# Keys and values of block 2 as seven products of half the columns, interleaved with the queries

## The chip, the cores and the metric

One core of one Trainium2 chip. The time is device microseconds (us) of one execution. Before the change three runs took 1544.66, 1544.93 and 1547.16 us, median 1544.93 us.

## The reference, cut to what matters

The program is two transformer blocks over 256 tokens of width 1,024, all in float32. Block 2 begins with a mixer whose input is projected to eight parts, among them the queries, keys and values of an attention; later comes a mixture of 64 experts.

```python
def mixer_block(u, cos, sin, w_in, conv_w, q_norm_g, k_norm_g, w_conv_out, w_attn_out, w_o):
    B, S, _ = u.shape
    proj = u @ w_in
    cb, cc, cx, q, k, v, gc, ga = split_columns(proj)
    ...
    q = rmsnorm(q.reshape(B, S, N_HEADS, HEAD_DIM), q_norm_g)
    k = rmsnorm(k.reshape(B, S, N_KV_HEADS, HEAD_DIM), k_norm_g)
    v = v.reshape(B, S, N_KV_HEADS, HEAD_DIM)
```

The queries have 1,024 columns, keys and values 256 each; `cc`, `cx`, `cb`, `gc`, `ga` have 1,024 each.

## The kernel before

**Seven products.** A product of a 256 x 1,024 activation with a 1,024 x 1,024 weight is cut into 2 x 2 blocks (tokens in halves of 128, the inner dimension in halves of 512, columns in halves of 512) and computed with seven block products in place of eight. With activation blocks a11, a12, a21, a22 (first index tokens) and weight blocks b11 to b22, DVE makes activation sums s1 = a21 + a22, s2 = s1 - a11, s3 = a11 - a21, s4 = a12 - s2 and weight sums t1 = b12 - b11, t2 = b22 - t1, t3 = b22 - b12, t4 = b21 - t2. PE makes product 1 = a11 b11, 2 = a12 b21, 5 = s1 t1, 6 = s2 t2, 7 = s3 t3, 3 = s4 b22, 4 = a22 t4, each four matmuls of 512 columns into one PSUM bank. The result blocks come from running sums: u2 = 1 + 6, u3 = u2 + 7, c22 = u3 + 5, c12 = u2 + (5 + 3), c21 = u3 + 4, c11 = 1 + 2. Product 2 is added by PE onto product 1 in its bank and 3 onto product 5, so product 2 waits until ACT has copied product 1 away, and product 3 waits until DVE has formed c22. Product 4 takes the bank of product 6 and waits for u2.

**The stretch of the change.** After block 1's last products (line 1432) the input of block 2 is normed, turned by PE (`norm_turn`, line 887) and scaled into `hT`, first for the first 128 tokens, then for the second. Keys and values, the unit `kv2` (512 columns, 2 MB), come as plain products in four parts of four matmuls (`part`, line 928): two parts on the first tokens, two on the second. DVE and ACT empty the two banks (`empty2`). Then come the queries as seven products in the order 1, 5, 6, 7, 2, 3, 4 (`q_seven`, line 1494, units `q0`, `q1`), then `cc` in the order 5, 1, 6, 7, 2, 3, 4 (`seven_product`, line 1553), then `cx`, `cb` with the attention between their products, then `gc`, `wco`, `ga`, `wao` (line 1558) and `wo`.

**Who sets the order.** Each engine runs a fixed list; `SCHEDULE2` gives the sequence of stages, and inside a stage it is the order of the calls. For the queries DVE runs `q_first_w_sums` (t1, t3, lines 2763 and 2764) and then `q_sums`: s1, s3, s2, t2, s4, t4 (lines 2771 to 2780), the rotation tables (2490), the norm and rotation of the keys (2511 to 2505), `cc`'s t1 (2554), `cc`'s t2 (2677), and only then the queries' u2, u3, c22 (all line 2799), `cc`'s t3 and t4 (2680, 2683), and c12 and c21.

**The ring.** Weights of 2 MB come through four slots. SP issues each unit's load (line 688) as soon as PE has counted up `dense_used` for the unit that had the slot before. `kv2` has slot 0, `q0` 1, `q1` 2, `cc0` 3, and `cc1` takes slot 0 after `kv2`. `kv2` is released in `q_seven`, right behind the first matmul of product 1:

```python
                        if product == 1 and c == 0:
                            release_last()
```

`release_last` waits until the last product of `kv2` is in its bank. `cc0` and `cc1` together hold b11 to b22 of `cc`, so its t1 needs both. The experts' 400 MB then come through 11 slots in the same way; the loads of the first ones wait for the end of the attention, of `wao` and of `wo`.

Of the kernel before, what the change touches and what calls it, by code (L numbers as in the profile page):

```python
# [168 lines left out]
SCHEDULE2 += [("part", "kv2", _q) for _q in range(4)] + [("seven", 0, 0)]  # L169
# [32 lines left out]
ORDER_UP = [1, 5, 6, 7, 2, 3, 4]  # L202
W_SUMS_UP = ["t1", "t3", "t2", "t4"]
# [17 lines left out]
def copied7(g):  # L221

    return 2 * SETS7 + g + (3 if g else 2)
# [22 lines left out]
def up_bank(m):  # L246

    return 4 * (m % 2)
# [10 lines left out]
def two_blocks(nc, t, out):  # L259

    with ExitStack() as ctx:
# [152 lines left out]
        q_t1, q_t3 = (flat1[:, at:at + 2048].rearrange("p (c n) -> p c n", c=4) for at in (0, 2048))  # L414
        q_x = flat1[:, 4096:6144].rearrange("p (j c s) -> p j c s", j=4, c=4)
# [61 lines left out]
        def up_seven_bank(m, product):  # L477
            return ps[:, up_bank(m) + BANK7[product], :]

# [117 lines left out]

        conv_mid, cbz_ready = sem("conv_mid"), sem("cbz_ready")
# [276 lines left out]
        def _(pe):  # L875
# [600 lines left out]
            def q_seven():  # L1476

                for n in ("q0", "q1"):
                    pe.wait_ge(dense_loaded[RING_SLOT[UNIT[n]]], dense_loads(UNIT[n]))
                b11, b12, b21, b22 = q_columns()  # L1480
                for product in ORDER_UP:
                    if product in (5, 6, 7, 4):
                        pe.wait_ge(w_sums7_ready, count7(-1, W_SUMS_UP, {5: "t1", 6: "t2", 7: "t3", 4: "t4"}[product]))
                    if product in (5, 6, 7, 3):
                        pe.wait_ge(x_sums7_ready, count7(-1, X_SUMS7, {5: "s1", 6: "s2", 7: "s3", 3: "s4"}[product]))
                    if product == 2:
                        pe.wait_ge(seven_copied, 2 * UP_SETS + 2)
                    if product in (3, 4):
                        pe.wait_ge(seven_sums, count7(-1, SUMS7, {3: "c22", 4: "u2"}[product]))
                    for c in range(4):  # L1490
                        lhs = {1: hT[:, c, 0:P], 2: hT[:, 4 + c, 0:P], 4: hT[:, 4 + c, P:S], 5: q_x[:, 0, c, :],
                               6: q_x[:, 1, c, :], 7: q_x[:, 2, c, :], 3: q_x[:, 3, c, :]}[product]
                        rhs = {1: b11, 2: b21, 3: b22, 4: w_sum_b, 5: q_t1, 6: b12, 7: q_t3}[product][:, c, :]
                        last = mm(ps[:, 4 + BANK7[product], :], lhs, rhs, start=(c == 0 and product not in (2, 3)),  # L1494
                                  stop=(c == 3), skip_group_check=True)
# [71 lines left out]
            def release_q():  # L1567

                pe.wait_ge(seven_filled, count7(-1, ORDER_UP, 4))
                pe.sem_inc(dense_used, 2)  # L1570
# [7 lines left out]
            for kind, a, q in SCHEDULE2:  # L1578
                if kind == "part":
                    if q % 2 == 0:  # L1580
                        wait_hT(16 + 2 * q)
                    part(a, hT, True, q)
                    if q == 0:
                        norm_turn(2, xn2, 1)
                elif kind == "product":
# [4 lines left out]
                elif kind == "seven":  # L1590
                    q_seven()
# [334 lines left out]
        def _(dve):  # L1926
# [548 lines left out]
            norm_rows(2, xn2, 0)  # L2475
            norm_take(2, 0)
            dve.wait_ge(ff_down, 5)
# [67 lines left out]
            def first_w_sums(g, part=(1, 3)):  # L2545
# [9 lines left out]
                if 3 in part:  # L2555
                    if SEVENS[g] == "cx":
                        dve.wait_ge(seven_filled, count7(-1, ORDER_UP, 4))
# [112 lines left out]
            def cc_w_sums(names):  # L2670

                b11, b12, b21, b22 = columns7(SET["cc"])
                for name in names:
                    if name == "t2":
                        dve.wait_ge(seven_filled, count7(-1, ORDER_UP, 5))
                        dve.wait_ge(w_sums7_ready, count7(0, W_SUMS_CC, "t1"))
                        v.tensor_tensor(q_t1, b22, w_sum_a, ALU.subtract).then_inc(w_sums7_ready, 1)
                    if name == "t3":
                        dve.wait_ge(seven_filled, count7(-1, ORDER_UP, 7))
                        v.tensor_tensor(q_t3, b22, b12, ALU.subtract).then_inc(w_sums7_ready, 1)  # L2680
# [85 lines left out]
            def q_sums():  # L2766
# [25 lines left out]
            def q_sum(name, dst, r, product):  # L2792

                dve.wait_ge(seven_filled, count7(-1, ORDER_UP, product))
                if name == "u2":
                    dve.wait_ge(seven_copied, 2 * UP_SETS + 2)
# [4 lines left out]
            dve.wait_ge(hT_act, 20)  # L2801
            q_first_w_sums()
            for kind, a, q in SCHEDULE2:
                if kind == "part":
                    if q % 2 and PRODUCTS[PROD[a]][1][q // 2] == "D":
                        empty2(a, q // 2)
                elif kind == "product":
# [232 lines left out]
        def _(act):  # L3040
# [208 lines left out]
            def empty2(name, bank):  # L3249
                b = filled_bank(name, bank)  # L3250
                if name == "kv2":
# [24 lines left out]
            for kind, a, q in SCHEDULE2:  # L3276
                if kind == "part":
                    if q % 2 and PRODUCTS[PROD[a]][1][q // 2] == "A":
                        empty2(a, q // 2)
                elif kind == "product":  # L3280
# [8 lines left out]
                elif kind == "seven":  # L3289
                    act.wait_ge(bank_emptied_dve, emptied("D", PROD["kv2"], 0))  # L3290
# [158 lines left out]
```

## Time and profile before

| what | value |
|---|---|
| median of three runs | 1544.93 us |
| profiled execution | 1545.07 us |
| its span on the core | 1543.2 us |
| PE busy | 1247.8 us (81%) |
| DVE busy | 549.4 us (36%) |
| ACT busy | 246.7 us (16%) |
| DMA, mean over the span | 325 GB/s |

The span is what the profiler saw of instructions; 1.87 us of the execution lie outside it. A float32 matmul shows as two records, so four matmuls read "x8". Start and end times are from the span's start. A bracket behind a timeline row is the idle time of that engine before it and what ended it.

### The profile page before, as it was taken

The numbers are of one execution on the slowest core, as the hardware profiler recorded it, in microseconds if no ns is written. First come the engines' busy times: TensorE is split into PE (matmuls) and PEld (weight loads), VectorE is DVE, ScalarE is ACT, GpSimd is POOL, SyncE is SP. The second block draws the span as 40 slices with busy tenths as digits, with TensorE's granted clock in tenths as the row PEclk, the third lists the DMA queues.
The fourth block names the chain that finished last, engine by engine and source line by source line (L and its number), as shares of the span: only waits on it lengthen the run. The fifth ranks groups of instructions, "written<-read, shape, count | busy, mean of one in ns | idle before, by whom it ended". The sixth has DMA issues, their size and how long they took to land.

```text
span 1543.2 us, 18891 instructions
## 1 busy us (share of the span) xinstructions
PE 1247.8 (81%) x8005; PEld 706.6 (46%) x8005; DVE 549.4 (36%) x1115; ACT 246.7 (16%) x710; POOL 18.2 (1%) x30
## 2 busy tenths in 40 slices
PE   8999999999999999996765775775676576577477
PEld 5665899944699544542232232232232233223223
DVE  6644578795756667421111111111111111111111
ACT  2434213211234101211010010010000001001001
POOL 2000000000000000100000000000000000000000
PEclk9999999999999999998888898788798789788889
DMA  9631746406433686999999999999999999999997
GB/s 305 217 111 55 244 153 217 162 30 217 163 112 113 236 303 237 374 429 428 429 429 429 428 429 428 428 429 428 429 429 428 428 429 428 429 429 429 429 426 327
DMA packets 93859, 501.53 MB, mean 325 GB/s; under 512 B 6845, under 2 KB 34865, under 8 KB 68464
## 3 DMA queue, kind: packets, MB, share of 16 engines
q1 hardware_dynamic: 93040, 500.00, 79.9%
q0 software_dynamic: 768, 0.85, 0.2%
q8 instruction: 33, 0.54, 0.1%
q14 instruction: 18, 0.15, 0.0%
HBM read 499.78 MB, written 1.05 MB: 325 GB/s over the span
## 4 chain that ended last, share of the span: by engine, by line
PE 58%; DMA 39%; DVE 2%; issue 1%; ACT 1%; SPq 0%; DVEq 0%
DMA arena<-in_w 38%; PE ps L1754 18%; PE ps L1329 8%; PE ps L1558 6%; PE ps L1553 4%; PE ps L1366 3%; PE ps L928 2%; PE ps L1139 2%; PE ps L933 2%; PE ps L978 2%; PE ps L1494 2%; PE ps L1654 1%; PE ps L1279 1%; PE ps L1432 1%; PE ps L955 0%
## 5 line engine op out<-in xcount | busy, mean ns | idle before, releaser
L1754 PE MATMUL ps<-arena,hT 128*32 128x512 f32 x1984 | 277.8, 723 | 252.7 <-DMA arena<-in_w 252.7
L1754 PEld LDWEIGHTS ps<-arena,hT 128*32 128x32 f32 x1984 | 69.2, 130 | 460.8 <-issue 319.3
L3006 DVE TENSOR_TENSOR moe_hid<-moe_hid,ps 64x512 f32<-64x512 f32 x32 | 22.1, 690 | 480.8 <-ACT moe_hid L3407 480.8
L1776 PE MATMUL ps<-arena,moe_turned 128*32 128x512 f32 x1024 | 118.3, 601 | 28.0 <-DVE moe_turned L3008 27.9
L1734 PEld LDWEIGHTS ps<-sel,h 128*128 128x128 f32 x992 | 113.2, 192 | 24.1 <-issue 24.1
L3407 ACT ACTIVATE moe_hid<-ps 64x512 f32<-64x512 f32 x32 | 18.8, 588 | 655.9 <-PE ps L1754 650.3
L1734 PE MATMUL ps<-sel,h 128*128 128x64 f32 x992 | 117.2, 276 | 0.0
L3391 ACT ACTIVATE hT<-ps,gcol 128x64 f32<-128x64 f32 x252 | 55.0, 328 | 156.8 <-PE ps L1734 156.8
L3008 DVE COPY moe_turned<-ps 128x512 f32<-128x512 f32 x32 | 22.1, 692 | 161.8 <-PE ps L1765 161.8
L1776 PEld LDWEIGHTS ps<-arena,moe_turned 128*32 128x32 f32 x1024 | 32.9, 110 | 88.7 <-issue 72.0
L1329 PE MATMUL ps<-arena 128*128 128x128 f32 x640 | 73.1, 275 | 0.0
L1329 PEld LDWEIGHTS ps<-arena 128*128 128x128 f32 x640 | 72.3, 192 | 0.0
L3010 DVE COPY moe_y<-ps 128x512 f32<-128x512 f32 x32 | 22.1, 692 | 125.0 <-PE ps L1776 125.0
L1785 PE MATMUL ps<-moe_y,moe_turned 64*128 64x512 f32 x256 | 63.6, 615 | 0.8 <-DVE moe_y L3010 0.8
L1558 PE MATMUL ps<-arena 128*128 128x512 f32 x144 | 63.7, 593 | 0.0
L1329 PE MATMUL ps<-hT,arena 128*128 128x128 f32 x480 | 55.4, 275 | 0.0
L1329 PEld LDWEIGHTS ps<-hT,arena 128*128 128x128 f32 x480 | 54.5, 192 | 0.0
L1553 PE MATMUL ps<-arena 128*128 128x128 f32 x384 | 44.7, 275 | 0.0
L1553 PEld LDWEIGHTS ps<-arena 128*128 128x128 f32 x384 | 44.3, 192 | 0.8 <-issue 0.5
L1366 PE MATMUL ps<-arena 128*128 128x512 f32 x96 | 42.4, 593 | 0.0
L1558 PEld LDWEIGHTS ps<-arena 128*128 128x128 f32 x144 | 27.0, 190 | 33.2 <-issue 32.0
L1785 PEld LDWEIGHTS ps<-moe_y,moe_turned 64*128 64x128 f32 x256 | 22.0, 186 | 42.8 <-issue 41.1
(499 smaller groups left out, 1427.3 us busy)
## 6 DMA issues: line engine op xcount, KB each, us to landing
arena<-in_w SPq DMA_DIRECT2D x182, 2048.0 KB, 29.4
arena<-in_w_in SPq DMA_DIRECT2D x18, 2048.0 KB, 9.1
arena<-in_w_up SPq DMA_DIRECT2D x22, 1024.0 KB, 9.0
arena<-in_w SPq DMA_DIRECT2D x17, 1024.0 KB, 12.9
arena<-in_w_down SPq DMA_DIRECT2D x5, 2048.0 KB, 13.5
arena<-in_w_out SPq DMA_DIRECT2D x2, 2048.0 KB, 15.2
arena<-in_w_conv_out SPq DMA_DIRECT2D x2, 2048.0 KB, 7.7
arena<-in_w_attn_out SPq DMA_DIRECT2D x2, 2048.0 KB, 11.9
```

Source lines behind the costliest of these rows:

```text
L928: last = mm(ps[:, at, :], xT[:, c, bank * P:(bank + 1) * P], w[:, c, :], start=(c == 0), stop=(c == KC - 1))
L933: last = mm(o, w[:, c, q * P:(q + 1) * P], xT[:, c, :], start=(c == 0), stop=(c == KC - 1))
L978: last = mm(ps[:, BANK1[product], :], lhs[:, c, :], rhs[:, c, :], start=(c == 0 and product != 3), stop=(c == 3), skip_group_check=True)
L1329: last = mm(up_seven_bank(m, product)[:, q * P:(q + 1) * P], wb[:, c, q * P:(q + 1) * P], xs[:, c, :], start=(new and q == 0 and c == 0), ...
L1366: return mm(ps[:, bank, :], x, w, start=(i == 0), stop=(i == NPAIR - 1))
L1553: last = mm(bank7(g, product)[:, m * P:(m + 1) * P], wb[:, c, m * P:(m + 1) * P], xs[:, c, :], start=(new and m == 0 and c == 0), stop=(c ...
L1558: last = mm(bank7(g, product), xs[:, c, :], wb[:, c, :], start=(new and c == 0), stop=(c == 3), skip_group_check=True)
L1734: last = mm(ps[:, GT, c * 2 * CAP:(c + 1) * 2 * CAP], hview[:, half, c, :], sel[:, half, :], start=(half == 0), stop=(half == 1))
L1754: last = mm(ps[k * CAP:(k + 1) * CAP, UP, :], x[:, c, (k % 2) * CAP:(k % 2 + 1) * CAP], w[:, at:at + DE], start=(c == 0), stop=(c == KC - 1))
L1776: last = mm(ps[k * CAP:(k + 1) * CAP, DN, :], a[:, m * 64 + (k % 2) * CAP:m * 64 + (k % 2 + 1) * CAP], w[:, at:at + 512], start=(m == 0), ...
L1785: last = mm(ps[:, 2 * half + n, :], sT[rows, half * P:(half + 1) * P], moe_y[rows, :], start=False, stop=False, skip_group_check=True)
L3391: return a_(xg[:, c, :], ps[:, bank, c * 2 * CAP:(c + 1) * 2 * CAP], ACT.Copy, scale=gcol[:, 3, c:c + 1])
```

## The change

Keys and values get seven products too, of 256 columns each: keys are the first column half, values the second. The activation sums s1 to s4 are those of the queries, made once, and now made ahead of the queries' weight sums. The weight sums of `kv2` (four of 128 x 1,024) are made by DVE during block 1's last products, into room of their own. PE runs, by `kv_and_queries`: kv 1, half of queries 1, the turn of the second tokens, the other half of queries 1, kv 2, then kv 5, 6, 7, queries 2, kv 3, kv 4, queries 5, 6, 7, 3, 4. ACT copies products 1 of both away first and takes the first tokens' keys and the queries' c11; DVE forms the other key and value blocks (`kv_sum`). `kv2` is now released behind the first matmul of the queries' product 5. The core of the diff:

```diff
-SCHEDULE2 += [("part", "kv2", _q) for _q in range(4)] + [("seven", 0, 0)]
+SCHEDULE2 += [("seven", 0, 0)]
...
+ORDER_Q, ORDER_KV = [1, 2, 5, 6, 7, 3, 4], [1, 2, 5, 6, 7, 3, 4]
...
-            def q_seven():
...
+            def kv(product):
...
+                if product == 1:
+                    u = UNIT["kv2"]
+                    pe.wait_ge(dense_loaded[RING_SLOT[u]], dense_loads(u))
+                    wait_bank(PROD["kv2"], 0)
+                    wait_bank(PROD["kv2"], 1)
+                b11, b12, b21, b22 = kv_columns()
+                if product in (5, 6, 7, 4):
+                    pe.wait_ge(kv_summed, count1(KV_SUMS, {5: "t1", 6: "t2", 7: "t3", 4: "t4"}[product]))
+                if product in (5, 6, 7, 3):
+                    pe.wait_ge(x_sums7_ready, count7(-1, X_SUMS7, {5: "s1", 6: "s2", 7: "s3", 3: "s4"}[product]))
+                if product == 2:
+                    pe.wait_ge(seven_copied, KV_COPIED)
+                if product in (3, 4):
+                    pe.wait_ge(kv_summed, count1(KV_SUMS, {3: "c22", 4: "u2"}[product]))
+                for c in range(4):
+                    lhs = {1: hT[:, c, 0:P], 2: hT[:, 4 + c, 0:P], 4: hT[:, 4 + c, P:S], 5: q_x[:, 0, c, :],
+                           6: q_x[:, 1, c, :], 7: q_x[:, 2, c, :], 3: q_x[:, 3, c, :]}[product]
+                    rhs = {1: b11, 2: b21, 3: b22, 4: kv_t["t4"], 5: kv_t["t1"], 6: kv_t["t2"], 7: kv_t["t3"]}[product][:, c, :]
+                    last = mm(kv_bank(product), lhs, rhs, start=(c == 0 and product not in (2, 3)), stop=(c == 3),
+                              skip_group_check=True)
+                last.then_inc(kv_filled, 1)
+
+            def queries(product, chunks=range(4)):
+
+                if product in (1, 5) and 0 in chunks:
+                    u = UNIT["q0" if product == 1 else "q1"]
...
-                        if product == 1 and c == 0:
-                            release_last()
...
+                    pe.wait_ge(x_sums7_ready, count7(-1, X_SUMS7, {5: "s1", 6: "s2", 7: "s3", 3: "s4"}[product]))
+                if product == 2:
+                    pe.wait_ge(seven_copied, KV_COPIED + 1)
...
+                    if product == 5 and c == 0:
+                        pe.wait_ge(kv_filled, len(ORDER_KV))
+                        pe.sem_inc(dense_used, 1)
+                if 3 in chunks:
                     last.then_inc(seven_filled, 1)
+
+            def kv_and_queries():
+
+                wait_hT(16)
+                kv(1)
+                queries(1, (0, 1))
+                norm_turn(2, xn2, 1)
+                queries(1, (2, 3))
+                kv(2)
+                wait_hT(20)
+                for product in (5, 6, 7):
+                    kv(product)
+                queries(2)
+                kv(3)
+                kv(4)
+                for product in (5, 6, 7, 3, 4):
+                    queries(product)
...
-                    q_seven()
+                    kv_and_queries()
...
+                x, y = {"t1": (b12, b11), "t3": (b22, b12), "t2": (b22, kv_t["t1"]), "t4": (b21, kv_t["t2"])}[name]
+                v.tensor_tensor(kv_t[name], x, y, ALU.subtract).then_inc(kv_summed, 1)
+
+            kv_w_sum("t1")
             norm_take(2, 0)
+            for name in ("t3", "t2", "t4"):
+                kv_w_sum(name)
...
-            def empty2(name, bank):
...
-                    v.tensor_copy(z2[:, 0, 1024:1280], b[:, 0:256])
-                    v.tensor_copy(v2[:, 0, :], b[:, 256:512]).then_inc(bank_emptied_dve, 1)
+            def kv_sum(name):
+
+                dst, r, product = {"u2": (kv_u2, kv_u2, 6), "u3": (kv_u3, kv_u2, 7), "c22": (v2[:, 1, :], kv_u3, 5),
+                                   "c12": (v2[:, 0, :], kv_u2, 3), "c21": (z2[:, 1, 1024:1280], kv_u3, 4)}[name]
+                dve.wait_ge(kv_filled, count1(ORDER_KV, product))
+                if name == "u2":
+                    dve.wait_ge(seven_copied, KV_COPIED)
+                else:
+                    dve.wait_ge(kv_summed, count1(KV_SUMS, {"u3": "u2", "c22": "u3", "c12": "u2", "c21": "u3"}[name]))
+                done = bank_emptied_dve if name == "c21" else kv_summed
+                v.tensor_tensor(dst, r, kv_bank(product), ALU.add).then_inc(done, 1)
...
+                dve.wait_ge(hT_act, 20)
                 v.tensor_tensor(q_x[:, 0], a21, a22, ALU.add).then_inc(x_sums7_ready, 1)
                 v.tensor_tensor(q_x[:, 2], a11, a21, ALU.subtract).then_inc(x_sums7_ready, 1)
                 dve.wait_ge(x_sums7_ready, count7(-1, X_SUMS7, "s1"))
                 v.tensor_tensor(q_x[:, 1], q_x[:, 0], a11, ALU.subtract).then_inc(x_sums7_ready, 1)
+                dve.wait_ge(x_sums7_ready, count7(-1, X_SUMS7, "s2"))
+                v.tensor_tensor(q_x[:, 3], a12, q_x[:, 1], ALU.subtract).then_inc(x_sums7_ready, 1)
+                q_first_w_sums()
+                for name in ("u2", "u3", "c22"):
+                    kv_sum(name)
                 dve.wait_ge(w_sums7_ready, count7(-1, W_SUMS_UP, "t3"))
                 v.tensor_tensor(b12, b22, q_t1, ALU.subtract).then_inc(w_sums7_ready, 1)
-                dve.wait_ge(x_sums7_ready, count7(-1, X_SUMS7, "s2"))
-                v.tensor_tensor(q_x[:, 3], a12, q_x[:, 1], ALU.subtract).then_inc(x_sums7_ready, 1)
                 dve.wait_ge(w_sums7_ready, count7(-1, W_SUMS_UP, "t2"))
                 v.tensor_tensor(w_sum_b, b21, b12, ALU.subtract).then_inc(w_sums7_ready, 1)
+                kv_sum("c12")
+                kv_sum("c21")
                 turn_tables()
                 keys()
                 first_w_sums(0, (1,))
...
-            dve.wait_ge(hT_act, 20)
-            q_first_w_sums()
...
-            def empty2(name, bank):
-                b = filled_bank(name, bank)
-                if name == "kv2":
-                    a_(z2[:, 1, 1024:1280], b[:, 0:256], ACT.Copy)
-                    a_(v2[:, 1, :], b[:, 256:512], ACT.Copy).then_inc(bank_emptied_act, 1)
...
+                    act.wait_ge(kv_filled, count1(ORDER_KV, 1))
+                    a_(kv_u2, kv_bank(1), ACT.Copy).then_inc(seven_copied, 1)
+                    act.wait_ge(seven_filled, count7(-1, ORDER_Q, 1))
+                    a_(r1_, ps[:, 4 + BANK7[1], :], ACT.Copy).then_inc(seven_copied, 1)
+                    act.wait_ge(kv_filled, count1(ORDER_KV, 2))
+                    a_(z2[:, 0, 1024:1280], kv_bank(2), ACT.Copy).then_inc(bank_emptied_act, 1)
+                    act.wait_ge(seven_filled, count7(-1, ORDER_Q, 2))
+                    a_(z2[:, 0, 0:512], ps[:, 4 + BANK7[2], :], ACT.Copy).then_inc(seven_copied, 1)
                     act.wait_ge(bank_emptied_dve, emptied("D", PROD["kv2"], 0))
...
-                    act.wait_ge(seven_filled, count7(-1, ORDER_UP, 1))
-                    a_(r1_, ps[:, 4 + BANK7[1], :], ACT.Copy).then_inc(seven_copied, 1)
                     act.wait_ge(seven_sums, count7(-1, SUMS7, "c22"))
                     head_squares(1, range(4, 8))
-                    act.wait_ge(seven_filled, count7(-1, ORDER_UP, 2))
-                    a_(z2[:, 0, 0:512], ps[:, 4 + BANK7[2], :], ACT.Copy).then_inc(seven_copied, 1)
-                    act.wait_ge(seven_copied, 2 * UP_SETS + 3)
+                    act.wait_ge(seven_copied, KV_COPIED + 2)
                     head_squares(0, range(4))
                     act.wait_ge(seven_sums, count7(-1, SUMS7, "c12"))
```

PE where `kv2` is released, the last two parts of keys and values and the start of the queries, before:

```order
L928 MATMUL ps<-arena,hT 128x512 [waits bank_emptied_dve,hT_act,hT_dve]
L928 MATMUL ps<-arena,hT 128x512 x7
L1494 MATMUL ps<-arena,hT 128x512 [waits dense_loaded2,dense_loaded1]
L1494 MATMUL ps<-arena,hT 128x512 [waits bank_filled]
L1494 MATMUL ps<-arena,hT 128x512 x2
L1494 MATMUL ps<-arena 128x512 [waits x_sums7_ready,w_sums7_ready]
L1494 MATMUL ps<-arena 128x512 x3
```

and now, from the queries' product 2 on (L1533 is the queries, L1511 keys and values):

```order
L1533 MATMUL ps<-arena,hT 128x512 [waits seven_copied]
L1533 MATMUL ps<-arena,hT 128x512 x3
L1511 MATMUL ps<-arena 128x256 [waits kv_summed,x_sums7_ready]
L1511 MATMUL ps<-arena 128x256 x3
L1511 MATMUL ps<-arena,hT 128x256 [waits kv_summed]
L1511 MATMUL ps<-arena,hT 128x256 x3
L1533 MATMUL ps<-arena 128x512 [waits x_sums7_ready,w_sums7_ready,dense_loaded2]
L1533 MATMUL ps<-arena 128x512 [waits kv_filled]
L1533 MATMUL ps<-arena 128x512 x2
```

The wait on `bank_filled`, behind which `kv2` is released, became one on `kv_filled`; the queries' products 1 and 2, which but for one matmul stood behind it, now stand in front of it.

PE at the end of the queries, products 7, 2, 3, 4, before:

```order
L1494 MATMUL ps<-arena 128x512 [waits x_sums7_ready,w_sums7_ready]
L1494 MATMUL ps<-arena 128x512 x3
L1494 MATMUL ps<-arena,hT 128x512 [waits seven_copied]
L1494 MATMUL ps<-arena,hT 128x512 x3
L1494 MATMUL ps<-arena 128x512 [waits seven_sums,x_sums7_ready]
L1494 MATMUL ps<-arena 128x512 x3
L1494 MATMUL ps<-arena,hT 128x512 [waits seven_sums,w_sums7_ready]
L1494 MATMUL ps<-arena,hT 128x512 x3
```

and now, products 7, 3, 4:

```order
L1533 MATMUL ps<-arena 128x512 [waits x_sums7_ready,w_sums7_ready]
L1533 MATMUL ps<-arena 128x512 x3
L1533 MATMUL ps<-arena 128x512 [waits seven_sums,x_sums7_ready]
L1533 MATMUL ps<-arena 128x512 x3
L1533 MATMUL ps<-arena,hT 128x512 [waits seven_sums,w_sums7_ready]
L1533 MATMUL ps<-arena,hT 128x512 x3
```

Product 2 went from between 7 and 3 to an earlier place; the wait of product 3 on `seven_sums` (for c22) now stands right behind product 7.

DVE from the last step of the keys' rotation, before (slot 0 is `dense_loaded0`; `moe_turned` is u2, `moe_hid` is u3, then c22):

```order
L2504 TENSOR_TENSOR arena<-arena 128x2x128 [waits dve_step]
L2505 TENSOR_TENSOR arena<-arena 128x2x128
L2554 TENSOR_TENSOR arena<-arena 128x2048 [waits dense_loaded0,dense_loaded3,dve_step]
L2677 TENSOR_TENSOR arena<-arena 128x2048 [waits w_sums7_ready,seven_filled]
L2799 TENSOR_TENSOR moe_turned<-moe_turned,ps 128x512 [waits seven_copied,seven_filled]
L2799 TENSOR_TENSOR moe_hid<-moe_turned,ps 128x512 [waits seven_sums,seven_filled]
L2799 TENSOR_TENSOR arena<-moe_hid,ps 128x512 [waits seven_sums,seven_filled]
```

and now:

```order
L2573 TENSOR_TENSOR arena<-arena 128x2x128 [waits dve_step]
L2574 TENSOR_TENSOR arena<-arena 128x2x128
L2629 TENSOR_TENSOR arena<-arena 128x2048 [waits dense_loaded0,dense_loaded3,dve_step]
L2752 TENSOR_TENSOR arena<-arena 128x2048 [waits w_sums7_ready,seven_filled]
L2880 TENSOR_TENSOR moe_turned<-moe_turned,ps 128x512 [waits seven_copied,seven_filled]
L2880 TENSOR_TENSOR moe_hid<-moe_turned,ps 128x512 [waits seven_sums,seven_filled]
L2880 TENSOR_TENSOR arena<-moe_hid,ps 128x512 [waits seven_sums,seven_filled]
```

Nothing moved here: the queries' u2, u3 and c22 stand behind `cc`'s t1, which waits for `cc1` in slot 0, as before.

## Rows read from the trace of the kernel before

**Rows 1.** The profile page, its 40 slices of 38.6 us: DMA share in tenths.

```profile
DMA  9631746406433686999999999999999999999997
```

**Rows 2.** Busy time by stretch: PE, PEld, DVE, ACT, POOL; then PE clock, DMA share, GB/s.

```profile
550.00:600.00 50.00, 50.00 (x119) 22.10 (x118) 32.08 (x29) 3.68 (x6) 0.00 (x0) 1.00 0.60 216
```

**Rows 3.** Chain of waits, 360 to 440 us and whole span: start, length, what, matmul records.

```profile
372.42 3.43 PE ps L928 x8
...
376.74 10.30 PE ps L928 x24
387.04 24.03 PE ps L1494 x56
411.07 25.01 PE ps L1553 x224
...
506.36 93.68 PE ps L1558 x218
```

**Rows 4.** Chain of waits, line 933: matmuls of 256 columns.

```profile
47.24 13.81 PE ps L933 x64
```

**Rows 5.** DMA issues of line 688: those of kv2 and q0, and the landing of each.

```profile
L688 SPq DMA_DIRECT2D arena<-in_w_in x1: 551/551/551, 353.6 to 353.6; - x1
L688 SPq DMA_DIRECT2D arena<-in_w_in x1: 546/546/546, 363.8 to 363.8; - x1
...
DMA to landing us min/median/max: 8.0/8.0/8.0
```

**Rows 6.** Issue of cc1 (line 688); landing of it, of the one at 411.2, of eleven (300 to 480 us).

```profile
387.16 0.54 SPq L688 DMA_DIRECT2D arena<-in_w_in  x1
...
DMA to landing us min/median/max: 9.2/9.2/9.2
...
DMA to landing us min/median/max: 9.6/9.6/9.6
...
DMA to landing us min/median/max: 7.8/8.7/14.4
```

**Rows 7.** Timeline of DVE, 352 to 412 us; start, length, instruction, idle before.

```profile
364.26 0.75 DVE L1952 TENSOR_SCALAR arena<-arena,rstd 128x1024 f32<-128x1024 f32 x1
...
372.46 0.69 DVE L2407 TENSOR_TENSOR arena<-arena,ps 128x512 f32<-128x512 f32 x1 [4.47 <-PE ps L1432]
...
377.95 2.29 DVE L2763 TENSOR_TENSOR arena<-arena 128x2048 f32<-128x2048 f32 x1 [0.49 <-ACT hT L3071]
...
382.36 0.42 DVE L2529 COPY arena<-ps 128x256 f32<-128x256 f32 x1
...
396.45 2.29 DVE L2554 TENSOR_TENSOR arena<-arena 128x2048 f32<-128x2048 f32 x1 [1.72 <-DMA arena<-in_w_in]
...
401.06 0.68 DVE L2799 TENSOR_TENSOR moe_turned<-moe_turned,ps 128x512 f32<-128x512 f32 x1
...
402.64 0.69 DVE L2799 TENSOR_TENSOR arena<-moe_hid,ps 128x512 f32<-128x512 f32 x1
```

**Rows 8.** Timeline of ACT, 352 to 412 us: scaling of the second tokens.

```profile
376.78 1.14 ACT L3071 ACTIVATE hT<-ps,gcol 128x128 f32<-128x128 f32 x4 [2.54 <-PE ps L887]
```

**Rows 9.** Timeline of PE, experts: three of the up products, line 1754.

```profile
701.60 7.08 PE L1754 MATMUL ps<-arena,hT 128*32 128x512 f32 x64 [1.76 <-DMA arena<-in_w]
...
730.80 9.69 PE L1754 MATMUL ps<-arena,hT 128*32 128x512 f32 x64 [11.03 <-DMA arena<-in_w]
...
760.32 8.59 PE L1754 MATMUL ps<-arena,hT 128*32 128x512 f32 x64 [8.93 <-DMA arena<-in_w]
```

**Rows 10.** Busy time by stretch, columns as in rows 2: where the clock changes.

```profile
722.00:723.00 1.00, 0.00 (x0) 0.00 (x0) 0.36 (x2) 0.00 (x0) 0.00 (x0) 0.74 1.00 426
756.00:757.00 1.00, 0.00 (x0) 0.00 (x0) 0.00 (x0) 0.00 (x0) 0.00 (x0) 0.80 1.00 426
736.00:737.00 1.00, 1.00 (x16) 0.35 (x12) 0.00 (x0) 0.00 (x0) 0.00 (x0) 0.94 1.04 442
```

**Rows 11.** Chain of waits, whole span: the last of 27 such gaps, behind its transfer.

```profile
1495.02 9.93 PE ps L1754 x64
```

More of the change, by code:

```diff
@@ L202 @@
 ORDER_UP = [1, 5, 6, 7, 2, 3, 4]
+ORDER_Q, ORDER_KV = [1, 2, 5, 6, 7, 3, 4], [1, 2, 5, 6, 7, 3, 4]
+KV_COPIED = 2 * UP_SETS + 2
+KV_SUMS = ["t1", "t3", "t2", "t4", "u2", "u3", "c22", "c12", "c21"]
 W_SUMS_UP = ["t1", "t3", "t2", "t4"]
@@ L221, in copied7 @@
 def copied7(g):
-    return 2 * SETS7 + g + (3 if g else 2)
+    return 2 * SETS7 + g + (4 if g else 3)
 def x_sum_wo(name):
@@ L414, in two_blocks @@
         q_t1, q_t3 = (flat1[:, at:at + 2048].rearrange("p (c n) -> p c n", c=4) for at in (0, 2048))
+        kv_t = {n: flat0[:, at:at + 1024].rearrange("p (c n) -> p c n", c=4)
+                for n, at in (("t1", 0), ("t2", 7168), ("t3", 8192), ("t4", 9216))}
+        kv_u2, kv_u3 = moe_y[:, 0:256], moe_y[:, 256:512]
         q_x = flat1[:, 4096:6144].rearrange("p (j c s) -> p j c s", j=4, c=4)
@@ L478, in up_seven_bank, with kv_bank, kv_columns @@
             return ps[:, up_bank(m) + BANK7[product], :]
+        def kv_bank(product):
+            return ps[:, BANK7[product], 0:256]
+        def kv_columns():
+            w = dense_slot("kv2").rearrange("p (c n) -> p c n", c=KC)
+            return w[:, 0:4, 0:256], w[:, 0:4, 256:512], w[:, 4:8, 0:256], w[:, 4:8, 256:512]
         def bank7(g, product):
@@ L1473, in attend @@
                         pe.sem_inc(attn2_done, 1)
-            def q_seven():
-                for n in ("q0", "q1"):
-                    pe.wait_ge(dense_loaded[RING_SLOT[UNIT[n]]], dense_loads(UNIT[n]))
-                b11, b12, b21, b22 = q_columns()
[L1481 to L1495, printed above, removed]
-                        if product == 1 and c == 0:
-                            release_last()
-                    last.then_inc(seven_filled, 1)
@@ new lines, in queries @@
+            def queries(product, chunks=range(4)):
+                if product in (1, 5) and 0 in chunks:
+                    u = UNIT["q0" if product == 1 else "q1"]
+                    pe.wait_ge(dense_loaded[RING_SLOT[u]], dense_loads(u))
+                b11, b12, b21, b22 = q_columns()
+                if product in (5, 6, 7, 4):
+                    pe.wait_ge(w_sums7_ready, count7(-1, W_SUMS_UP, {5: "t1", 6: "t2", 7: "t3", 4: "t4"}[product]))
+                if product in (5, 6, 7, 3):
+                    pe.wait_ge(x_sums7_ready, count7(-1, X_SUMS7, {5: "s1", 6: "s2", 7: "s3", 3: "s4"}[product]))
+                if product == 2:
+                    pe.wait_ge(seven_copied, KV_COPIED + 1)
+                if product in (3, 4):
+                    pe.wait_ge(seven_sums, count7(-1, SUMS7, {3: "c22", 4: "u2"}[product]))
+                for c in chunks:
+                    lhs = {1: hT[:, c, 0:P], 2: hT[:, 4 + c, 0:P], 4: hT[:, 4 + c, P:S], 5: q_x[:, 0, c, :],
+                           6: q_x[:, 1, c, :], 7: q_x[:, 2, c, :], 3: q_x[:, 3, c, :]}[product]
+                    rhs = {1: b11, 2: b21, 3: b22, 4: w_sum_b, 5: q_t1, 6: b12, 7: q_t3}[product][:, c, :]
+                    last = mm(ps[:, 4 + BANK7[product], :], lhs, rhs, start=(c == 0 and product not in (2, 3)),
+                              stop=(c == 3), skip_group_check=True)
+                    if product == 5 and c == 0:
+                        pe.wait_ge(kv_filled, len(ORDER_KV))
+                        pe.sem_inc(dense_used, 1)
+                if 3 in chunks:
+                    last.then_inc(seven_filled, 1)
@@ L1567, in release_q @@
             def release_q():
[L1569 removed]
+                pe.wait_ge(seven_filled, count7(-1, ORDER_Q, 4))
                 pe.sem_inc(dense_used, 2)
@@ L1578, in _ @@
             for kind, a, q in SCHEDULE2:
[L1579 to L1585, printed above, removed]
+                if kind == "product":
                     seven_product(SET[a], q, hT, release_q if a == "cc" else lambda: release_seven(SET[a] - 1))
@@ L2792, in q_sum @@
             def q_sum(name, dst, r, product):
-                dve.wait_ge(seven_filled, count7(-1, ORDER_UP, product))
+                dve.wait_ge(seven_filled, count7(-1, ORDER_Q, product))
                 if name == "u2":
-                    dve.wait_ge(seven_copied, 2 * UP_SETS + 2)
+                    dve.wait_ge(seven_copied, KV_COPIED + 1)
                 else:
@@ L2799, in q_sum @@
                 v.tensor_tensor(dst, r, ps[:, 4 + BANK7[product], :], ALU.add).then_inc(seven_sums, 1)
-            dve.wait_ge(hT_act, 20)
-            q_first_w_sums()
             for kind, a, q in SCHEDULE2:
[L2804 to L2807, printed above, removed]
+                if kind == "product":
                     if a == "cc":
@@ L3276, in _ @@
             for kind, a, q in SCHEDULE2:
[L3277 to L3280, printed above, removed]
+                if kind == "product":
                     if q == 1:
```

18 lines of the change are left out of this document (13 added, 5 removed).

## The prediction

> **What bounds the kernel now.** I read four views in this order. The page's slices first: the DMA share is full from slice 18 on and patchy before it [rows 1], so the experts are bound by their weights and all else by something other than transfers. Second the busy time by stretch, just ahead of that point: 550 to 600 us has PE busy for all of its 50 us at full clock with DMA at 0.60 [rows 2]. Third the chain of waits: from 372.42 us it is PE without a hole, keys and values, then queries, then `cc`; and one piece of line 1558 alone, `gc` to `wao`, runs for 93.68 us [rows 3]. So block 2's mixer is bound by PE, and each load of the experts starts on an event of PE's list. A microsecond more or less between 372 and 411 us moves everything behind it by the same, the full stream of weights too: no load is in flight when the queries end that could take up the difference, and up to 600 us DMA has room. I count the end one for one. Last I read SP and DVE in this stretch, since the change moves what they wait for.
>
> **PE's own work.** Before, keys and values cost 3.43 + 10.30 = 13.73 us, the queries 24.03 us, 3.43 for each product [rows 3]. Now keys and values are 28 matmuls of 256 columns, 56 records; 64 such records took 13.81 us in another stage [rows 4], so 56 cost 12.08 us, 1.73 a product. That removes **1.65 us**. The queries' matmuls stay 28.
>
> **What DVE and ACT gain in work** hides, I think. Four weight sums of 128 x 1,024 come to DVE; one of 128 x 2,048 took 2.29 us [rows 7], so one costs some 1.2 us. The first follows the norm that ends at 365.01, and the row behind the other three shows DVE idle for 4.47 us, up to 372.46 [rows 7]; three sums are 3.6 us. `kv2`, issued at 353.6, landed 8.0 us later, at 361.6 [rows 5], so the first doesn't wait. If that cover were gone, the norm of the second tokens would be late by what is over, which nothing suggests beyond a few tenths. Queries 1 now starts at 374.15 and needs `q0`: issued at 363.8, landed at 371.8 [rows 5]. Kv 2 starts at 378.46 and needs ACT's copy of kv 1. ACT is done with `hT` at 377.92 [rows 8], and a copy of that size takes 0.42 us on DVE [rows 7]: just in time. Kv 5 needs s1, which DVE can start at 377.95, where it started the queries' first weight sum before [rows 7]; kv 5 comes at 380.18. Further on DVE makes the queries' t1 and t3, two sums of 2.29 us, and then u2, u3, c22 of kv at some 0.5 us each: done by about 386.5, and kv 3 comes at 388.80. I cost all of this at nothing.
>
> **PE's new times**, if nothing waits: kv 1 and half of queries 1 from 372.42 to 375.87, the turn to 376.76 (0.89 us between the two pieces of line 928 [rows 3]), half of queries 1 and kv 2 to 380.2, kv 5, 6, 7 to 385.4, queries 2 to 388.8, kv 3 and 4 to **392.25**, queries 5, 6, 7 to **402.55**.
>
> **What is late next: `cc1`.** `kv2` is released when kv 4 is done, behind queries 1 and 2, at 392.25 and not at 387.04. SP issued `cc1` 0.12 us after that point, at 387.16 [rows 3, 6]; now 392.37. It landed 9.2 us later, at 396.36, and DVE, which had been idle for 1.72 us for it, began `cc`'s t1 at 396.45 [rows 6, 7]. Behind that in DVE's fixed order stand `cc`'s t2 and then the queries' u2, u3 and c22, the last from 402.64 to 403.33 [rows 7]: 16.17 us from issue to c22. Before, PE had product 2 to run between 7 and 3, and product 3 began at 404.2 (two products of 3.43 ahead of 411.07 [rows 3]), after c22. Now product 3 follows 7 directly. With the same 16.17 us c22 is there at 408.54, and PE, free at 402.55, stands for **6.0 us**. The cost's bounds come from the landing: eleven loads of this kind took 7.8 to 14.4 us [rows 6], the long ones queued behind others; with nothing else in flight I take 9.2, the same load's own row, and as ends 7.8 and the 9.6 of the next load to an idle queue, issued at 411.2 [rows 6]. That is a stall of 4.6 to 6.4 us.
>
> The Trainium skill, "DMA: Bandwidth & Descriptors", in its cost model (fixed and variable component), gives about 2.0 us plus the bytes at 436 GB/s. For 2 MB that is an estimate of 6.8 us, and by it the stall would be some 3.6 us and the sum +2.0 us at full clock. The trace disagrees: no load of this size landed in under 7.8 us [rows 6].
>
> **The clock.** PE has not stood this long anywhere ahead of the experts. There it does, waiting for weights, and the clock goes with it. The gap ahead of 730.80 began at 719.77, and the granted clock falls from 2.4 to 1.2 GHz within 722 to 723 us (mean 0.74); the one ahead of 760.32 began at 751.39, and it falls within 756 to 757 us (0.80) [rows 9, 10]: after 2.7 and 5.2 us without a matmul. After the restart at 730.80 the clock is back within 736 to 737 us (0.94) [rows 10]. The same 64 records cost 7.08 us where the gap was 1.76 us, and 9.69, 8.59 and 9.93 behind long gaps [rows 9, 11]: 1.5 to 2.9 us dearer, 2.3 in the mean. A stall of 6.0 us is longer than either fall took, so I charge product 3 and 4 with **2.2 us**; zero is the other end, for a stall that ends before the clock falls. That gives no cost to others: DVE's sums t3 and t4 of `cc` (4.6 us) fit beside products 3 and 4.
>
> **Sum.** -1.65 + 6.0 + 2.2 = **+6.6 us**. Behind `cc`'s first product all engines stand to each other as before; `q0` and `q1` are released there, and `cx`'s loads move with it. The profiled execution took 1545.07 us, which is 0.14 above the median, so I forecast 1551.7 us.
>
> **The rivals.**
> *Stall, but no fall of the clock.* `cc1` lands sooner, or PE restarts ahead of the fall. For it: the two gaps differ by 2.5 us in when the clock fell, and the median of the eleven loads is 8.7 us [rows 6]. Against it: the load's own row says 9.2. It gives -1.65 + 4.6 to 6.0, so +3.0 to +4.4 us: 1548.0 to 1549.5.
> *No change.* The load of `cc1` doesn't decide, because it lands before DVE comes to it. Then product 3 still waits for u3 and c22, which read product 7: from u2 to c22 there were 1.58 us for two steps [rows 7], so u3 and c22 cost about 1.5 us behind 402.55, and c22 is there at 404.1. That takes back the 1.65: 1545.0. It decides if `cc1` lands by 397.1, since c22 ends 6.97 us after the landing; that is 4.7 us after the issue, against 7.8 for the fastest of eleven. So it needs a release some 3 us earlier than I read the order.
> *Faster.* The 1.65 us are kept whole, 1543.4, if product 3 doesn't have to wait at all. Product 3 adds onto 5 in its bank, so the wait on c22 is there; only an error in my reading leaves this.
> *Worse.* A second wait in the new part (kv 2 on ACT, the norm on the weight sums), or a later landing, up to a few us more: 1553 and above.
>
> **How the numbers follow.** About 0.2%, 3.1 us, is what a measurement of this kernel can tell from no change. Stall with the clock's fall 0.70; stall without it 0.16, of which a little lies within 3.1 us; no change 0.07; faster 0.03; worse 0.04. Slower thus 0.89, within 0.08, faster 0.03. The range reaches from the shortest stall at full clock, +3.0, to the longest with the dearest restart, -1.65 + 6.4 + 2.9 = +7.7: 1548.0 to 1552.8.
>
> **What would show it.** In the profile after: 56 records of kv of some 0.216 us and no hole up to 402.5 us; the DMA issue of `cc1` at about 392.4; DVE idle until 401.6, waiting for that DMA; PE idle for some 6 us ahead of the queries' product 3, ended by DVE's c22; the granted clock at 0.5 in the microseconds around 408 to 412; `cc` starting at 417.6 in place of 411.07, and the experts' stream shifted by the same. The prediction is wrong if `cc1` is issued near 387 us, if PE's gap is below 4 us, or if the shift at `cc` isn't found again at the end.

## The result and the profile after

| | before | after |
|---|---|---|
| median, 7 runs each | 1545.63 us | 1551.37 us |
| span of the profiled execution | 1543.2 us | 1549.4 us |
| ratio to before, 95% interval | | 1.0034 (1.0024 to 1.0044) |
| PE busy | 1247.8 us | 1251.1 us |
| DVE busy | 549.4 us | 555.6 us |

The change made the kernel 5.7 us slower, where +6.6 was forecast. In the changed kernel's file the queries are line 1533, keys and values 1511, `cc` 1611, the queries' u2 to c22 line 2880 and `cc`'s t1 line 2629. PE's timeline of the stretch:

```profile
371.83 1.89 PE L1511 MATMUL ps<-arena,hT 128*128 128x256 f32 x8
...
377.87 1.95 PE L1511 MATMUL ps<-arena,hT 128*128 128x256 f32 x8
379.65 5.34 PE L1511 MATMUL ps<-arena 128*128 128x256 f32 x24
384.83 3.60 PE L1533 MATMUL ps<-arena,hT 128*128 128x512 f32 x8
388.26 1.89 PE L1511 MATMUL ps<-arena 128*128 128x256 f32 x8
389.99 1.89 PE L1511 MATMUL ps<-arena,hT 128*128 128x256 f32 x8
391.72 10.46 PE L1533 MATMUL ps<-arena 128*128 128x512 f32 x24
407.21 5.37 PE L1533 MATMUL ps<-arena 128*128 128x512 f32 x8 [5.03 <-DVE arena L2880]
412.41 3.60 PE L1533 MATMUL ps<-arena,hT 128*128 128x512 f32 x8
415.84 3.73 PE L1611 MATMUL ps<-arena 128*128 128x128 f32 x32
```

Up to 402.18 us PE has no hole: the saving is there. Then it stands for 5.03 us until DVE's line 2880 is done, and product 3, which should take 3.60 us as its neighbour does, takes 5.37. What stood behind this is on SP and DVE, in SP's timeline, the landing in the view of its source line, and DVE's timeline:

```profile
392.00 0.54 SPq L703 DMA_DIRECT2D arena<-in_w_in  x1
```

```profile
DMA to landing us min/median/max: 8.1/8.1/8.1
```

```profile
396.98 0.42 DVE L2574 TENSOR_TENSOR arena<-arena 128x256 f32<-128x256 f32 x1
400.19 2.29 DVE L2629 TENSOR_TENSOR arena<-arena 128x2048 f32<-128x2048 f32 x1 [2.79 <-DMA arena<-in_w_in]
402.58 2.29 DVE L2752 TENSOR_TENSOR arena<-arena 128x2048 f32<-128x2048 f32 x1
404.79 0.68 DVE L2880 TENSOR_TENSOR moe_turned<-moe_turned,ps 128x512 f32<-128x512 f32 x1
405.58 0.69 DVE L2880 TENSOR_TENSOR moe_hid<-moe_turned,ps 128x512 f32<-128x512 f32 x1
406.37 0.69 DVE L2880 TENSOR_TENSOR arena<-moe_hid,ps 128x512 f32<-128x512 f32 x1
```

`cc1` is issued at 392.00 in place of 387.16 [rows 6]; DVE has nothing to do from 397.40 to 400.19, since the next thing in its list wants that load, and the sums that PE wants stand behind it. The clock, in the busy time by stretch (the third number from the right is the granted share of 2.4 GHz):

```profile
407.00:408.00 1.00, 0.79 (x1) 0.47 (x2) 1.00 (x2) 0.91 (x7) 0.00 (x0) 0.62 0.00 0
408.00:409.00 1.00, 1.00 (x2) 0.34 (x1) 1.00 (x1) 0.97 (x7) 0.00 (x0) 0.50 0.02 8
410.00:411.00 1.00, 1.00 (x3) 0.40 (x2) 1.00 (x1) 0.00 (x0) 0.00 (x0) 0.67 0.00 0
411.00:412.00 1.00, 1.00 (x4) 0.40 (x3) 0.59 (x1) 0.00 (x0) 0.00 (x0) 1.00 0.00 0
```

It falls to 1.2 GHz just as PE gets its data back and rises within 410 to 411 us. The shift then goes down the chain of waits unchanged; the piece of 93.68 us, at 506.36 us before [rows 3], now reads:

```profile
511.29 93.68 PE ps L1616 x218
```

That is 4.93 us later with the same length: the 5.36 us worked out below, less the 0.43 by which this execution reached the stretch earlier. One thing has to be taken out when traces are compared: where keys and values begin varies by up to 3.4 us between executions, before anything that the change touches (372.42 us before, 371.99 after, both in the chain of waits; by PE's timeline 371.16 in e2 and 374.52 in e4 below). So I compare the **distance from the first matmul of keys and values to the first of `cc`**: 411.07 - 372.42 = 38.65 us before [rows 3] (410.91 - 372.26 by the timeline, the same), 415.84 - 371.83 = 44.01 us after, which is +5.36.

### The profile page after: what moved, and what is told of

It reads as the page before. It is cut to its first block, busy times and chain, and to the rows that moved or that the text cites. A ratio compares the mean times of both kernels' runs of the same rounds, so it can differ in the third digit from the quotient of the medians.

```text
span 1549.4 us, 18956 instructions
## 1 busy us (share of the span) xinstructions
PE 1251.1 (81%) x8029; PEld 711.3 (46%) x8029; DVE 555.6 (36%) x1122; ACT 247.0 (16%) x710; POOL 18.2 (1%) x30
## 4 chain that ended last, share of the span: by engine, by line
PE 57%; DMA 38%; DVE 2%; issue 1%; ACT 1%; SPq 0%; PEld 0%; DVEq 0%; PEldq 0%
DMA arena<-in_w 37%; PE ps L1806 18%; PE ps L1344 8%; PE ps L1616 6%; PE ps L1611 4%; PE ps L1381 3%; PE ps L1154 2%; PE ps L948 2%; PE ps L993 2%; PE ps L1706 1%; DMA arena<-in_w_in 1%; PE ps L1828 1%; PE ps L943 1%; PE ps L1294 1%; PE ps L1533 1%
## 5 line engine op out<-in xcount | busy, mean ns | idle before, releaser
L1828 PE MATMUL ps<-arena,moe_turned 128*32 128x512 f32 x1024 | 123.0, 623 | 27.8 <-DVE moe_turned L3084 27.8
```

What stands on the lines that cost most here:

```text
L1828: last = mm(ps[k * CAP:(k + 1) * CAP, DN, :], a[:, m * 64 + (k % 2) * CAP:m * 64 + (k % 2 + 1) * CAP], w[:, at:at + 512], start=(m == 0), ...
```

## The experiments

The theory: `kv2`'s slot is freed late, so `cc1` lands late; DVE waits for it with the queries' sums behind; PE waits for those; and the clock falls in that wait. Rivals: product 2 is missing as a cover between 7 and 3; or the new products' own work (DVE's nine sums, the waits between kv products) costs the time. Nine kernels tell them apart. "+" is against the kernel before, timed on the same chip; distances are from the timelines of PE.

**e1: the sums first.** DVE's list alone is changed:

```diff
                 keys()
-                first_w_sums(0, (1,))
-                cc_w_sums(("t2",))
                 q_sum("u2", r2_, r1_, 6)
                 q_sum("u3", r3_, r2_, 7)
                 q_sum("c22", z2[:, 1, 512:1024], r3_, 5)
+                first_w_sums(0, (1,))
+                cc_w_sums(("t2",))
```

> One edit to the changed kernel: on DVE the queries' u2, u3 and c22 go ahead of cc's t1 and t2. The late-load theory: product 3 of the queries no longer stands behind the landing of cc1; it waits for u3 and c22 alone, some 1.5 us behind product 7 (5.0 in the changed kernel), too short for the clock to fall; cc starts near 410.6 us of the span and the time is that of the kernel before, within 1 us. A rival, that the added work of the new products is what costs: the time stays some 5.5 us above the kernel before. Another rival, that product 2 is missing between 7 and 3: the stall stays near 5 us.

Measured: 1545.29 us against 1545.26, ratio 1.0000 (0.9991 to 1.0009). PE's timeline around product 3:

```profile
394.36 10.46 PE L1533 MATMUL ps<-arena 128*128 128x512 f32 x24
406.49 3.67 PE L1533 MATMUL ps<-arena 128*128 128x512 f32 x8 [1.67 <-DVE arena L2880]
```

This execution began keys and values at 374.46; the distance to `cc` is 38.97 us, 0.3 above before. The stall is 1.67 us, that of u3 and c22 alone, and the clock stays up. The load came just as late (issued at 394.64, 20.18 us behind the first matmul; 392.00 - 371.83 = 20.17 in the changed kernel), but PE's sums no longer stood behind it. All the new work is in this kernel, so the new work isn't what costs.

**e2: product 2 back between 7 and 3.** Product 5 takes its place ahead of kv 3; ACT's copy of the queries' first block moves along, and the release of `kv2` stands behind the first matmul of product 6, held by kv 4 as before.

```diff
-                queries(2)
+                queries(5)
                 kv(3)
                 kv(4)
-                for product in (5, 6, 7, 3, 4):
+                for product in (6, 7, 2, 3, 4):
```

> One edit to the changed kernel: product 2 of the queries goes back to between 7 and 3, and product 5 takes its place ahead of kv 3 and 4; kv2 is released behind kv 4 as in the changed kernel, at the same time. The rival that product 2 is missing as cover: stall gone, time 1.6 us below the kernel before. The late-load theory: PE reaches product 3 at the same 402.2 us, since it has the same work ahead of it, and c22 comes no sooner: a stall of 5 to 6 us ahead of product 3 with the fall of the clock, time 5 to 6.5 us above the kernel before.

Measured: 1551.58 us against 1545.26, ratio 1.0043 (1.0029 to 1.0057), distance 44.66 us, 6.01 above before.

PE's timeline:

```profile
397.92 3.60 PE L1533 MATMUL ps<-arena,hT 128*128 128x512 f32 x8
406.63 5.92 PE L1533 MATMUL ps<-arena 128*128 128x512 f32 x8 [5.12 <-DVE arena L2880]
```

The stall is 5.12 us with product 2 right ahead of it. `cc1` was issued at 391.34, 20.18 us behind the first matmul. Product 2 is no cover here: PE has the same work ahead of product 3 in either order, and c22 comes when the load lets it. That rival falls.

**e3: both edits.**

> Both edits: queries' sums ahead of cc's t1 on DVE, and product 2 between 7 and 3. The late-load theory: u3 and c22 lie beside product 2, cc's t1 is ready at 402 to 404 us, well ahead of cc; no stall is left and the 1.65 us of PE work are kept: time 1.6 us below the kernel before (about 1544.0), cc starting near 409 us. The rival that the new products themselves cost: 5 us above.

Measured: 1543.94 us against 1545.26, ratio 0.9989 (0.9980 to 0.9998).

PE's timeline, from kv 1, then products 2, 3, 4 and the start of `cc`:

```profile
371.33 1.89 PE L1511 MATMUL ps<-arena,hT 128*128 128x256 f32 x8
...
398.09 3.60 PE L1533 MATMUL ps<-arena,hT 128*128 128x512 f32 x8
401.52 3.60 PE L1533 MATMUL ps<-arena 128*128 128x512 f32 x8
404.96 3.60 PE L1533 MATMUL ps<-arena,hT 128*128 128x512 f32 x8
408.39 3.73 PE L1611 MATMUL ps<-arena 128*128 128x128 f32 x32
```

No hole is left; the distance is 37.06 us, 1.59 below before. So the seven products do bring what they save on PE, 1.65 by the rows, once u3 and c22 have product 2 beside them and no load ahead of them. Either edit alone doesn't do it: e1 lacks the cover, e2 keeps the load. This version beats both kernels, the one before by 1.3 us, with an interval that just leaves out no change.

**e7 and e4: a later release that wasn't one.** In e7 the kernel before releases `kv2` behind the first matmul of the queries' product 6, in e4 the changed kernel does (the diff is that of e7; in e4 it is 6 in place of 5):

```diff
-                        if product == 1 and c == 0:
+                        if product == 6 and c == 0:
                             release_last()
```

> The kernel before with one edit: kv2 is released behind the first matmul of the queries' product 6 in place of product 1, some 6.9 us later; keys and values stay plain. The late-load theory: cc1 is issued near 394 us, c22 comes at 409 to 410.3, PE stands for 4.9 to 6 us ahead of product 3 (at 404.2), the clock falls for 1.8 to 2.2 us more: 6.7 to 8.2 us above the kernel before. The rivals (order of products, or the new products' own work): no change, since neither is in this kernel.

> The changed kernel with kv2 released behind the first matmul of the queries' product 6 in place of 5: 3.4 us later, nothing else. The late-load theory: the stall ahead of product 3 grows one for one, to 8 to 9.2 us, with one fall of the clock as before: 8.3 to 9.8 us above the kernel before. If the load didn't decide, the time stays at the changed kernel's.

Measured: e7 1544.54 us, ratio 0.9996 (0.9986 to 1.0005), distance 38.65, as before to the digit. e4 1553.40 us, ratio 1.0045 (1.0028 to 1.0062), distance 43.77 us, as the changed kernel. Its time, 7.3 us above the kernel before, says less: its four executions lie at 1552.5 and 1554.3, and the profiled one, 1554.24, began keys and values at 374.52. Both miss, and SP's timeline says why (e7, then e4):

```profile
386.31 0.54 SPq L688 DMA_DIRECT2D arena<-in_w_in  x1
```

```profile
394.70 0.54 SPq L703 DMA_DIRECT2D arena<-in_w_in  x1
```

In e7 the load is issued at 386.31, though the release stands behind nine matmuls that run until 393.6. What held it were the waits ahead of it in PE's list: the last matmul of `kv2` ends at 386.10 (`bank_filled`), and product 6, behind whose first matmul the release stands, waits for t2, which DVE ends at 386.17:

```profile
383.89 2.28 DVE L2776 TENSOR_TENSOR arena<-arena 128x2048 f32<-128x2048 f32 x1
```

So the release came 0.14 us after the last of these waits, and 7.3 us before the matmuls ahead of it had run. In e4 it is the same: the load is issued 0.12 us after kv 4 is done, as in the changed kernel, and 3 us before the matmul ahead of the release starts. The release isn't late in either kernel, so they say nothing of the theory, and the two were made again with a wait.

**e9 and e8: a later release that is held.** As e7 and e4, with one line more (here that of e9; in e8 the same wait replaces the one on `kv_filled`):

```diff
-                        if product == 1 and c == 0:
+                        if product == 6 and c == 0:
+                            pe.wait_ge(seven_filled, count7(-1, ORDER_UP, 5))
                             release_last()
```

> As e7, the kernel before with a later release of kv2 and nothing else, now held until the queries' product 5 is in its bank, so that it does come late: cc1 issued near 394.0 us, c22 at 409.1 to 410.3, PE stands for 4.9 to 6 us ahead of product 3, the clock falls for 1.5 to 2.2 us more: 6.4 to 8.2 us above the kernel before. The rivals (order of products, or the new products' own work): no change, since neither is in this kernel.

> As e4, but the release behind the first matmul of the queries' product 6 now waits until product 5 is in its bank; in e4 it had only the place in the list, and PE's sequencer came past it long before the matmuls ran. The late-load theory: cc1 is issued some 3.5 us later than in the changed kernel (395.4 where keys and values start at 372), the stall ahead of product 3 is 8.4 to 9.5 us in place of 5.0, one fall of the clock as before, cc starts 8.6 to 10.1 us later than in the kernel before, and the time is that much longer. If the load didn't decide: as the changed kernel.

Measured: e9 1552.38 us against 1545.04, ratio 1.0046 (1.0030 to 1.0063), distance 45.34 us, +6.69. PE around product 3:

```profile
399.59 3.60 PE L1494 MATMUL ps<-arena,hT 128*128 128x512 f32 x8
408.19 5.11 PE L1494 MATMUL ps<-arena 128*128 128x512 f32 x8 [5.00 <-DVE arena L2800]
```

Plain keys and values, the old order, and still the same picture as after the change, from the late load alone: issued at 393.01, a stall of 5.00 us behind product 2, product 3 at 5.11. The added wait itself opened no hole on PE, whose rows run on to 403.19. e8 1555.66 us, ratio 1.0069 (1.0052 to 1.0085), +10.6, distance 47.72, +9.07; the distance lies in the range expected, the time 0.5 above it:

```profile
410.97 5.83 PE L1533 MATMUL ps<-arena 128*128 128x512 f32 x8 [8.28 <-DVE arena L2880]
```

`cc1` was issued 23.60 us behind the first matmul in place of 20.17, 3.43 later; the stall grew from 5.03 to 8.28, by 3.25, with a landing of 7.9 in place of 8.1 us. So the stall follows the release one for one.

**e6: an earlier release.** Kv 3 and 4 ahead of the queries' product 2, the release behind product 2's first matmul.

```diff
-                queries(2)
                 kv(3)
                 kv(4)
-                for product in (5, 6, 7, 3, 4):
+                for product in (2, 5, 6, 7, 3, 4):
```

> The changed kernel with kv 3 and 4 ahead of the queries' product 2, kv2 released right behind them: PE waits about 1.0 us for kv's c22, the release comes 2.4 us sooner (389.5 us). The late-load theory: the stall ahead of product 3 shrinks to 1.5 to 2.6 us and the clock doesn't fall: 0.9 to 2.0 us above the kernel before. If the load didn't decide, the added wait of 1 us makes it 1 us slower than the changed kernel.

Measured: 1548.87 us against 1546.12, ratio 1.0022 (1.0012 to 1.0032), distance 40.98 us, +2.33.

```profile
387.21 1.96 PE L1511 MATMUL ps<-arena 128*128 128x256 f32 x8 [1.16 <-DVE arena L2603]
...
406.92 3.67 PE L1533 MATMUL ps<-arena 128*128 128x512 f32 x8 [2.29 <-DVE arena L2879]
```

PE's timeline shows two short waits, 1.16 us for kv's c22 and 2.29 for the queries', in place of one of 5.03, and product 3 at 3.67: no fall of the clock. By the distance it is 0.3 us above the range expected, by the time 0.75. DVE's timeline shows what the theory left out here:

```profile
396.71 0.18 DVE L2579 RECIPROCAL arena<-arena 128x4 f32<-128x4 f32 x1 [2.83 <-ACT arena L3368]
399.91 2.29 DVE L2628 TENSOR_TENSOR arena<-arena 128x2048 f32<-128x2048 f32 x1
```

`cc1` was issued at 391.03 and landed 8.0 us later, at 399.0, but DVE came to `cc`'s t1 only at 399.91: ACT copies the queries' product 2 ahead of its part of the keys' norm, that product now comes later, and DVE's keys stood 2.83 us for ACT. The load was issued 2.03 us sooner, c22 came only 1.3 us sooner, and the rest by which the stall shrank, 1.4 us, is PE's coming later to product 3. So e6 shows the direction, and not the release one for one.

**e5: PE kept busy in the stall.** Five matmuls of 512 columns into a free bank, whose result nobody reads:

```diff
                 for product in (5, 6, 7, 3, 4):
+                    if product == 3:
+                        for _ in range(5):
+                            mm(ps[:, 3, :], hT[:, 0, 0:P], hT[:, 0:2, :].rearrange("p c s -> p (c s)"), start=True, stop=True)
                     queries(product)
```

> The changed kernel with five matmuls of 512 columns, whose result nobody reads, between the queries' products 7 and 3: some 4.3 us of PE work inside the stall. It adds work and takes nothing away. If the clock's fall costs its 1.8 us apart from the stall: the granted clock stays at 2.4 GHz, product 3 takes 3.6 us in place of 5.4, it starts when c22 is there as before, and the time is 1.8 us below the changed kernel, 3.6 to 4 above the kernel before. If the fall costs nothing (hidden behind other work), no change against the changed kernel.

Measured: 1548.51 us against 1546.12, ratio 1.0019 (1.0009 to 1.0029), distance 42.27 us, 1.74 below the changed kernel and 3.62 above the kernel before, as expected; by the times it is 2.4 above, less than expected.

```profile
401.42 4.45 PE L1558 MATMUL ps<-hT 128*128 128x512 f32 x10
406.55 3.67 PE L1533 MATMUL ps<-arena 128*128 128x512 f32 x8 [0.68 <-DVE arena L2883]
```

Its busy time by stretch at the same place:

```profile
406.00:407.00 1.00, 0.45 (x1) 0.30 (x2) 1.00 (x2) 0.56 (x4) 0.00 (x0) 1.00 0.00 0
407.00:408.00 1.00, 1.00 (x4) 0.46 (x3) 1.00 (x1) 0.97 (x8) 0.00 (x0) 1.00 0.03 8
```

Product 3 starts when c22 is there, 35.33 us behind the first matmul against 35.38 in the changed kernel, so the stall is the same; only the clock is another, and product 3 takes 3.67 us and not 5.37. Work that nobody needs made the kernel faster than the changed one by the distances; the intervals of the two ratios overlap between 1.0024 and 1.0029, so the times alone would not prove it. The fall of the clock is a term of its own, 1.7 us of the 5.4.

## Why the prediction was right

Against the distance of the kernel before:

| term | forecast | measured | where |
|---|---|---|---|
| PE's own work | -1.65 | -1.59 | e3, no hole left |
| stall ahead of product 3 | +6.0 | +5.03 | bracket of product 3 |
| fall of the clock | +2.2 | +1.74 | changed kernel less e5 |
| sum | +6.6 | +5.2 | distance +5.36, times +5.74 |

The 0.18 us between the sum and the distance are a seam of the rows: a row of matmuls ends 0.17 us after the next one starts (384.83 + 3.60 against 388.26), and the bracket counts from that end.

- **What bounds, and one for one:** right. The 93.68 us of line 1616 moved by 4.93 us without change, and e9 and e8 show shifts of 6.7 and 9.1 us at `cc` that come out in the times as 7.3 and 10.6; what the times hold beyond the shift is told below. (By [rows 1] DMA is full from the 17th slice on, not the 18th; nothing hangs on it.)
- **PE's work and what hides:** right. All the new work on DVE and ACT was covered; PE ran from kv 1 to product 7 without a hole, to 402.18 us, where 402.55 was forecast from a start 0.43 later.
- **`cc1`:** the mechanism was right, the size a little off. The step that was mis-sized is "I take 9.2, the same load's own row": the load landed in 8.1 us here and in 7.9 to 8.2 us in e1 to e9, so the 9.2 of the kernel before was the dear case, and the lower end of 7.8 the nearer one. These 1.1 us account for the difference between 6.0 and 5.03. The estimate of 6.8 us, from the cost model in the Trainium skill, "DMA: Bandwidth & Descriptors", section "Anatomy of one DMA", is still below every row. The Trainium skill fits that model there on loads that GpSimd issues, and these are SP's, so the rows don't contradict it; they show that the figure doesn't carry over. The prediction's floor of 7.8 us holds for its eleven rows alone: several other 2 MB loads of that trace landed in 7.7, and the shortest in all traces took 7.5 us (e5 and e7).
- **The clock:** right that it falls, and near in size. With a stall of 5.03 us it was close: it fell just when PE restarted. It fell in all the other traces with a stall of 5 us or more, e2, e4, e8 and e9, in e2 within 404 to 405 us and in e8 within 405 to 406, well ahead of the restart at 406.63 and 410.97; in e1 and e6, with 1.67 and 2.29 us, it stayed at 2.4 GHz.
- **The rivals:** "no change" was e1: the same stall of u3 and c22, 1.67 us where about 1.5 was forecast, that takes back the 1.65. It needed no earlier release but another order on DVE. "Faster" was e3.

Two things outside the stretch blur the times, and are why the terms above are judged by distances; in e4 the two differ by 2.2 us. The first is at the end. The shift holds up to the start of the experts' last down product, 4.80 us, and that product then takes 1.35 us more (before, then after):

```profile
1531.75 3.99 PE L1776 MATMUL ps<-arena,moe_turned 128*32 128x512 f32 x32 [0.78 <-DVE moe_turned L3008]
1536.55 5.34 PE L1828 MATMUL ps<-arena,moe_turned 128*32 128x512 f32 x32 [0.78 <-DVE moe_turned L3084]
```

The clock in a microsecond of each, before and after:

```profile
1533.00:1534.00 1.00, 1.00 (x16) 0.26 (x8) 0.00 (x0) 0.00 (x0) 0.00 (x0) 1.00 0.08 33
1538.00:1539.00 1.00, 1.00 (x12) 0.22 (x6) 0.00 (x0) 0.00 (x0) 0.00 (x0) 0.50 0.06 25
```

This product takes some 4 us in the kernel before, e1, e5 and e7, and 5.3 in the other seven traces, e3 and e9 among them. So it goes neither with the new products nor with the time; what decides it isn't shown.

The second is at the start: why keys and values begin up to 3.4 us later in some executions can in part be read from the traces. In e1 and e4, the two latest, the clock stood at 1.2 GHz from 92 to 98 us, in block 1, which the change doesn't touch; the same 16 records take 3.72 us in the trace after and 5.39 in e1:

```profile
94.55 3.72 PE L948 MATMUL ps<-hT,arena 128*128 128x256 f32 x16
95.53 5.39 PE L948 MATMUL ps<-hT,arena 128*128 128x256 f32 x16
```

and the clock in e1:

```profile
95.00:96.00 1.00, 1.00 (x7) 0.67 (x4) 0.95 (x5) 1.00 (x5) 0.00 (x0) 0.50 0.76 204
```

From there on e1 is 2.65 us behind. No wait in the trace explains this fall: the largest idle time in PE's timeline from 58 to 92 us is 0.33 us, in e1 as in the trace after. What sets it off stays open, and was not tried.

## What to carry to other kernels

When a product is cut up and interleaved with its neighbour, its weights stay in use longer: look up who gets their slot, and which engine's list has that load's wait in it, before counting the matmuls saved. In a list that runs in order, work for which another engine waits should not stand behind a wait for a load that is needed later; moving three sums ahead of two turned a loss of 5.7 us into none, and with one product moved as well into a gain of 1.3 us. A stall of some 5 us on PE cost 1.7 us more than itself, since the clock fell in it; the two waits of e6, 1.16 and 2.29 us, cost nothing beyond themselves.

## What the runs showed that I had not expected

In e7 and e4 PE carried out a release as soon as the waits up to it in its list were over, and not when the matmuls ahead of it had run: in e7, behind nine matmuls, 7.7 us of work, it came 0.14 us after the last of these waits, and in e4 3 us before the matmul ahead of it started. The place of the release in PE's list set no time there; a wait did.
